# A two-layer hybrid trunk on one core: the routing stretch ahead of the experts written in another order, and a 15th place in the ring of expert weights

## The reference, cut to what matters

```python
def reference(x, ...):                       # x: (1, 256, 1024) float32
    for i in range(2):
        h = rms_norm(x, norm_g[i, 0])
        y = pool_mixer(h, ...) if i % 2 == 0 else forgetting_attention(h, ...)
        x = x + rms_norm(y, norm_g[i, 1])
        h = rms_norm(x, norm_g[i, 2])
        y = swiglu(h, ...) if i % 2 == 0 else moe_swiglu(h, ...)
        x = x + rms_norm(y, norm_g[i, 3])

def moe_swiglu(h, w_router, w_gate, w_up, w_down):
    logits = h @ w_router                    # (256, 8)
    top_val, top_idx = lax.top_k(logits, 2)
    top_w = softmax(top_val)
    gates = sum(one_hot(top_idx, 8) * top_w[..., None])
    for e in range(8):                       # w_gate[e], w_up[e]: 1024 x 3584; w_down[e]: 3584 x 1024
        out = out + gates[..., e:e+1] * ((silu(h @ w_gate[e]) * (h @ w_up[e])) @ w_down[e])
```

## Time and profile before

| what | value |
|---|---|
| median of 3 runs | 1231.81 us (1231.67 to 1235.57) |
| profiled execution: its own time | 1235.62 us |
| profiled execution: span of the trace | 1233.8 us |
| PE busy | 1201.3 us, 97% of the span |
| DVE busy | 686.5 us, 56% |
| ACT busy | 539.6 us, 44% |
| mean DMA rate over the span | 335 GB/s |
| chain of work that ended last | PE 85%, DVE 7%, DMA 6% |

### The profile page before, as it was taken

One profiled execution on the slowest core, in us unless ns is written; L12 is line 12 of the kernel. 1 busy time (PEld: TensorE's weight loads), 2 busy tenths in 40 slices (PEclk: granted clock), 3 DMA queues, 4 the chain that ended last, 5 costly groups with the idle time before them and its releaser, 6 DMA issues.

```text
span 1233.8 us, 15258 instructions
## 1 busy us (share of the span) xinstructions
PE 1201.3 (97%) x5922; PEld 845.5 (69%) x5922; DVE 686.5 (56%) x761; ACT 539.6 (44%) x525; POOL 144.0 (12%) x141
## 2 busy tenths in 40 slices
PE   9999999989989999999999999999999999999996
PEld 8888887778878888434788833578883357887332
DVE  4844455646577988101888710288861038895102
ACT  3743334445546776002677500267750036774001
POOL 0000000000025460100006020000602000050200
PEclk9999999999989999999999999999999999999999
DMA  9955553653376999899999999999999999999994
GB/s 296 361 184 192 180 195 116 198 185 109 109 279 244 370 364 366 334 420 421 422 422 421 419 393 419 423 422 423 419 408 392 420 422 423 422 419 387 397 421 189
DMA packets 128279, 413.52 MB, mean 335 GB/s; under 512 B 10753, under 2 KB 30209, under 8 KB 113794
## 3 DMA queue, kind: packets, MB, share of 16 engines
q1 hardware_dynamic: 127394, 409.28, 85.2%
q0 software_dynamic: 816, 3.28, 0.8%
HBM read 411.48 MB, written 1.05 MB: 334 GB/s over the span
## 4 chain that ended last, share of the span: by engine, by line
PE 85%; DVE 7%; DMA 6%; ACT 1%; SPq 1%; issue 1%; DVEq 0%; ACTq 0%
PE bank L1480 19%; PE bank L1482 19%; PE bank L1481 19%; PE bank L1862 14%; DMA raw<-in_moe_w_gate 5%; PE bank L1875 4%; DVE raw_lo L972 3%; PE bank L1814 1%; PE bank L1942 1%; PE bank L1896 1%; PE bank L1487 1%; SPq L582 1%; DMA head_row<-in_heads 1%; PE bank L1738 1%; DVE y L1391 1%
## 5 line engine op out<-in xcount | busy, mean ns | idle before, releaser
L972 DVE TENSOR_TENSOR raw_lo<-raw,w_hi 128x2048 fp32r<-128x2048 f32 x148 | 337.9, 2303 | 72.1 <-ACT w_hi L641 71.6
L641 ACT ACTIVATE w_hi<-raw 128x2048 fp32r<-128x2048 f32 x149 | 284.5, 1917 | 122.1 <-PE bank L1482 75.7
L1480 PE MATMUL bank<-w_hi,h_hi 128*128 128x512 f32 x568 | 226.4, 399 | 9.8 <-DVE h_lo L1335 5.3
L1481 PE MATMUL bank<-raw_lo,h_hi 128*128 128x512 f32 x576 | 225.0, 391 | 0.0
L1482 PE MATMUL bank<-w_hi,h_lo 128*128 128x512 f32 x568 | 222.6, 392 | 0.0
L1862 PE MATMUL bank<-raw,h_b 128*64 128x512 f32 (+1 forms) x768 | 143.1, 523 | 0.0
L1480 PEld LDWEIGHTS bank<-w_hi,h_hi 128*128 128x128 f32 x568 | 107.1, 189 | 40.7 <-issue 11.5
L1481 PEld LDWEIGHTS bank<-raw_lo,h_hi 128*128 128x128 f32 x576 | 108.7, 189 | 21.9
L1482 PEld LDWEIGHTS bank<-w_hi,h_lo 128*128 128x128 f32 x568 | 106.9, 188 | 23.2
L972 DVE TENSOR_TENSOR raw_extra_lo<-raw_extra,w_hi 128x2048 fp32r<-128x2048 f32 x48 | 112.9, 2372 | 14.6 <-ACT w_hi L641 14.4
L1862 PEld LDWEIGHTS bank<-raw,h_b 128*64 128x64 f32 x768 | 53.6, 137 | 82.5 <-issue 73.9
(11 more groups left out here) (320 smaller groups left out, 1624.4 us busy)
## 6 DMA issues: line engine op xcount, KB each, us to landing
raw<-in_moe_w_gate SPq DMA_DIRECT2D x96, 1024.0 KB, 13.6
raw<-in_moe_w_up SPq DMA_DIRECT2D x80, 1024.0 KB, 14.4
raw<-in_moe_w_down SPq DMA_DIRECT2D x64, 1024.0 KB, 13.9
raw_extra<-in_moe_w_down SPq DMA_DIRECT2D x48, 1024.0 KB, 16.1
raw_extra<-in_moe_w_up SPq DMA_DIRECT2D x32, 1024.0 KB, 12.5
raw_extra<-in_moe_w_gate SPq DMA_DIRECT2D x16, 1024.0 KB, 10.4
raw<-in_ffn_w_gate SPq DMA_DIRECT2D x11, 1024.0 KB, 5.3
raw<-in_ffn_w_up SPq DMA_DIRECT2D x11, 1024.0 KB, 5.0
```

The lines of the kernel that those rows point to most:

```text
L641: nc.scalar.activation(to, raw_slot(source), ACT.Copy).then_inc(hi_ready, 1)
L972: nc.vector.tensor_tensor(lo_slot(source), raw_slot(source), high.bitcast(f32), ALU.subtract).then_inc(lo_ready, 1)
L1480: mm(out, a_hi, b_hi, start=first, stop=False)
L1481: mm(out, a_hi, b_lo, start=False, stop=False)
```

## The change

It has two parts. The first writes the routing in another order: `mboth` is marked for both blocks at once, the gain multiplication of `xn` moves for three quarters from POOL to DVE, the whole low part of the first unit comes behind `sel`, the experts' order and the gates are worked out behind the low part of the first expert's fourth unit and beyond, POOL clears `y` only when the first tokens are split (`he_lo_done` 2), and the router's and the ranking's products repeat their 8 columns 16 times to make 128. The counts of `keep_warm` change. The second gives the ring a 15th place, over `h_lo`, which is free when the attention's projections are done; the split tokens move to `h_e`, over `h_hi`. 84 units are not a multiple of 15 places, and the places are dealt out afresh for each pair (unit j of a pair has place j % 15).

```diff
-EXTRA_SLOTS = 4
+EXTRA_SLOTS = 5
...
-EXPERT_RING = [j % (RAW_SLOTS + EXTRA_SLOTS) for j in range(ROUND_UNITS)]
-assert ROUND_UNITS % (RAW_SLOTS + EXTRA_SLOTS) == 0
+PAIR_UNITS = 2 * ROUND_UNITS
+EXPERT_RING = [j % (RAW_SLOTS + EXTRA_SLOTS) for j in range(PAIR_UNITS)]
...
-WARM = (8, 6, 0, 8, 0, 4, 6)
+WARM = (8, 6, 4, 4, 3, 5, 6)
...
+        with nc.sbuf_tensor("h_e", [P, 2, KB, P], f32r) as h_e:
+            pass
...
-        with nc.sbuf_tensor("x_sq", [P, TB, D], f32) as x_sq:
+        with nc.sbuf_tensor("raw_h", [P, UNIT], f32) as raw_h:
+            pass
+        with nc.sbuf_tensor("raw_h_lo", [P, UNIT], f32r) as raw_h_lo:
             pass
...
-            place = EXPERT_RING[j % ROUND_UNITS]
+            place = EXPERT_RING[j % PAIR_UNITS]
...
         def moe_last(j):
 
-            return max(i for i in range(j - ROUND_UNITS, j) if moe_slot(i) == moe_slot(j))
+            return max(i for i in range(j - PAIR_UNITS, j) if moe_slot(i) == moe_slot(j))
...
         def raw_slot(s):
-            return raw[:, s, :] if s < RAW_SLOTS else raw_extra[:, s - RAW_SLOTS, :]
+            if s == RAW_SLOTS:
+                return raw_h[:, :]
+            return raw[:, s, :] if s < RAW_SLOTS else raw_extra[:, s - RAW_SLOTS - 1, :]
...
-                    sp.wait_ge(*[(unit_used, OUT_U0 + 1), (unit_used, MOE_U0), (x_done, 6),
+                    sp.wait_ge(*[(unit_used, OUT_U0), (unit_used, OUT_U0 + 1), (unit_used, MOE_U0), (x_done, 6),
                                  (x_done, 6)][EXPERT_RING[j] - RAW_SLOTS])
...
-                nc.scalar.activation((x_sq if n == 6 else xn)[:, tb, :], x[:, tb, :], ACT.Square,
+                    sc.wait_ge(sq_done, sq_at(6, 0))
+                nc.scalar.activation(ye[:, :] if n == 6 else xn[:, tb, :], x[:, tb, :], ACT.Square,
...
-
-            def lo_half(u, half):
-                cols = slice(half * (UNIT // 2), (half + 1) * (UNIT // 2))
-                ve.wait_ge(hi_ready, u + 1 - WHOLE_UNITS)
-                step = nc.vector.tensor_tensor(lo_slot(slot_of(u))[:, cols], raw_slot(slot_of(u))[:, cols],
-                                               hi_slot(u)[:, cols].bitcast(f32), ALU.subtract)
-                if half == 1:
-                    step.then_inc(lo_ready, 1)
...
-            def top_two(tb):
+            def top_found(tb):
                 ve.wait_ge(lg_psum, tb + 1)
                 link(nc.vector.tensor_copy(lg[:, tb, :], bank[4 + tb][:, 0:E]))
                 link(nc.vector.max(top[:, tb, :], lg[:, tb, :]))
                 link(nc.vector.max_index(topi[:, tb, :], top[:, tb, :], lg[:, tb, :]))
-                link(nc.vector.tensor_copy(topf[:, tb, :], topi[:, tb, 0:2]))
-                for i in range(2):
-                    step = nc.vector.tensor_scalar(m12[:, tb, i, :], iota8, topf[:, tb, i:i + 1], None, ALU.is_equal)
-                link(step)
-                nc.vector.tensor_tensor(mboth[:, tb, :], m12[:, tb, 0, :], m12[:, tb, 1, :],
-                                        ALU.add).then_inc(m_done, 1)
-
-            top_two(0)
-            lo_half(MOE_U0, 0)
-            top_two(1)
+
+            top_found(0)
+            gain_landed(6)
+            nc.vector.tensor_tensor(xn[:, 1, :], x[:, 1, :], gain[:, 0, :], ALU.mult).then_inc(xn_done, 1)
+            nc.vector.tensor_tensor(xn[:, 0, HALF:D], x[:, 0, HALF:D], gain[:, 0, HALF:D], ALU.mult).then_inc(xn_done, 1)
+            top_found(1)
+            link(nc.vector.tensor_copy(topf[:, :, :], topi[:, :, 0:2]))
+            link(nc.vector.tensor_tensor(m12[:, :, :, :], iota8[:, None, None, :].to_broadcast([P, TB, 2, E]),
+                                         topf[:, :, :, None].to_broadcast([P, TB, 2, E]), ALU.is_equal))
+            nc.vector.tensor_tensor(mboth[:, :, :], m12[:, :, 0, :], m12[:, :, 1, :], ALU.add).then_inc(m_done, 1)
             root(6, 0, TB)
-            ve.wait_ge(m_done, 2)
+            ve.wait_ge(m_done, 1)
             link(nc.vector.tensor_scalar(away[:, :, :], mboth[:, :, 0:1], float(-2 * T), float(2 * T),
                                          ALU.mult, ALU.add))
 
             ve.wait_ge(rank_psum, 1)
...
             link(nc.vector.tensor_tensor(pos0[:, :, :], rank_ps[:, :, 0:1], away[:, :, :], ALU.add))
             for tb in range(TB):
                 nc.vector.tensor_scalar(sel[:, tb, :], iota, pos0[:, tb, :], rstd[:, 6, tb:tb + 1],
                                         ALU.is_equal, ALU.mult).then_inc(sel_ready, 1)
-            lo_half(MOE_U0, 1)
+            lo(MOE_U0)
+            nc.vector.tensor_copy(rank[:, :, :], rank_ps).then_inc(rank_copied, 1)
+            ve.wait_ge(rank_psum, 2)
+            nc.vector.tensor_copy(count, bank[4][:, 0:E]).then_inc(rank_copied, 1)
...
@@ -1332,8 +1339,8 @@
             def he_lo(p, ahead=0, halves=range(2)):
                 for i in halves:
                     ve.wait_ge(he_hi_done, p * 2 + (2 * ahead + i + 1))
-                    nc.vector.tensor_tensor(h_lo[:, 4 * i:4 * i + 4, 0:P], bank_blocks(3, 6 + i),
-                                            h_hi[:, 4 * i:4 * i + 4, 0:P].bitcast(f32),
+                    nc.vector.tensor_tensor(h_e[:, 1, 4 * i:4 * i + 4, :], bank_blocks(3, 6 + i),
+                                            h_e[:, 0, 4 * i:4 * i + 4, :].bitcast(f32),
                                             ALU.subtract).then_inc(he_lo_done, 1)
...
 
-            ve.wait_ge(rank_psum, 2)
-            link(nc.vector.scalar_tensor_tensor(key, count, float(E), tie, ALU.mult, ALU.add))
-            link(nc.vector.tensor_tensor(ahead[:, :, :], key[:, None, :].to_broadcast([P, E, E]),
...
-            link(nc.vector.tensor_tensor_scan(incl, big, big, 0.0, ALU.add, ALU.bypass))
-            nc.vector.tensor_scalar(rtab_i[:, 0:1], incl[0:1, E - 1:E], float(PAIRS), None,
-                                    ALU.add).then_inc(pairs_done, 1)
             lo(MOE_U0 + 3)
-            nc.vector.tensor_copy(rank[:, :, :], rank_ps).then_inc(rank_copied, 1)
-            ve.wait_ge(gexp_done, 1)
-            link(nc.vector.tensor_scalar(gtmp[:, :, 2:3], gtmp[:, :, 1:2], 1.0, None, ALU.add))
-            link(nc.vector.reciprocal(gate[:, :, 0:1], gtmp[:, :, 2:3]))
-            nc.vector.tensor_tensor(gate[:, :, 1:2], gate[:, :, 0:1], gtmp[:, :, 1:2], ALU.mult).then_inc(gates_done, 1)
...
+            def shares():
+                ve.wait_ge(rank_copied, 2)
+                link(nc.vector.scalar_tensor_tensor(key, count, float(E), tie, ALU.mult, ALU.add))
...
+                link(nc.vector.tensor_scalar(small, place, float(PAIRS), None, ALU.is_ge))
+
+            def shares_rest():
+                link(nc.vector.tensor_scalar(cap, small, float(CAP_B - CAP), float(CAP), ALU.mult, ALU.add))
...
+                nc.vector.tensor_scalar(rtab_i[:, 0:1], incl[0:1, E - 1:E], float(PAIRS), None,
+                                        ALU.add).then_inc(pairs_done, 1)
+
+            def gate_shares():
+                ve.wait_ge(gexp_done, 1)
...
+                if is_pair(p, 0):
+                    shares()
+                    lo_to(AHEAD)
+                    shares_rest()
+                    lo_to(AHEAD + 2)
+                    gate_shares()
                 lo_to(last_up(0) + 2)
                 gated_halves(0)
...
+                    if tb == 1:
+                        keep_warm(WARM[2 + 2 * i])
                     pe.wait_ge(*((x_done, 5), (x_done, 5), (x_front, 1), (x_done, 6))[2 * tb + i])
...
+            def repeated(columns):
+                return columns[:, None, :].to_broadcast([P, P // E, E])
+
             def router(tb):
                 for k in range(KB):
                     if k % 4 == 0:
                         pe.wait_ge(x_t_done, 2 * tb + k // 4 + 1)
-                    step = mm(bank[4 + tb][:, 0:E], x_t[:, k, tb * P:(tb + 1) * P], wr_g[:, k, :], start=(k == 0),
-                              stop=(k == KB - 1))
+                    step = mm(bank[4 + tb][:, 0:P], x_t[:, k, tb * P:(tb + 1) * P], repeated(wr_g[:, k, :]),
+                              start=(k == 0), stop=(k == KB - 1))
...
             keep_warm(WARM[5])
 
-            pe.wait_ge(m_done, 2)
+            pe.wait_ge(m_done, 1)
             ones, before = consts[:, C_ONES:C_ONES + P], consts[:, C_TRIS:C_TRIS + P]
-            mm(bank[5][:, 0:E], before, mboth[:, 0, :], start=True, stop=True)
-            mm(bank[5][:, E:2 * E], ones, mboth[:, 0, :], start=True, stop=False)
-            mm(bank[5][:, E:2 * E], before, mboth[:, 1, :], start=False, stop=True).then_inc(rank_psum, 1)
-            mm(bank[4][:, 0:E], ones, mboth[:, 0, :], start=True, stop=False)
-            mm(bank[4][:, 0:E], ones, mboth[:, 1, :], start=False, stop=True).then_inc(rank_psum, 1)
+            both = [repeated(mboth[:, tb, :]) for tb in range(TB)]
+            mm(bank[5][:, 0:P], before, both[0], start=True, stop=True)
+            mm(bank[5][:, P:2 * P], ones, both[0], start=True, stop=False)
```

(40 more changed lines are left out.)

38 lines of the change are left out of this document (20 added, 18 removed).

## The result

The changed kernel takes 1218.2 us (median of four runs, 1216.9 to 1219.5); the kernel before takes 1232.7 on the same chip. The ratio is 0.9876, 95% interval 0.9853 to 0.99, so between 12 and 18 us faster. The forecast was 1221. The profiled execution took 1219.5 us, with a span of 1217.7.

A forecast was written before the change was run, and what follows sets the result against it. PE and DMA were taken as near balance, ring depth deciding, with the routing waiting on small DVE steps. Routing 8.0, 15th place 5.3 and clock 1.5 took 14.8 us off 1235.62: 1220.8, set at 1221, range 1216.5 to 1227.5.

The forecast's parts named there:

- The routing's length: Routing up to the first expert: PE starts it at 368.5 in place of 375.83, gain 7.3 us.
- POOL's first step: Routing, root of block 1: POOL's multiplication of xn, halved to 512 columns, lets DVE's addition end earlier, gain 0.85 us.
- POOL's second step: Routing, search and marks: POOL's second multiplication, 2.36 us, lies over DVE's cast, 1.89 us, and compares, 2.39 us.
- The 15th place: Three changes from "b" to "a" experts: one more unit in flight removes PE's waits, gain 5.3 us, lower end 2.5.
- the sum: Whole kernel: 8.0 + 5.3 + 1.5 = 14.8 us off the profiled 1235.62, giving 1220.8; median set at 1221.
- The clock term: Behind the third change: PE at clock 0.50 from 1011 to 1014 us, half lost, counted as 1.5 us gained.
- The 0.7 us behind the third unit: First expert: PE's wait at 384.69, 0.7 us behind three units' end, came from the experts' order and goes.
- The lead on landing: At the three changes: units land some 7 to 8 us before PE's first product.
- The slower rival: Ring places dealt out afresh: unit 84 waits for unit 75, PE stands 6.5 us at each change, 1241.8; chance 0.05.
- The clearing: First expert: POOL's clearing of y beside DVE's low parts; forecast 0 us, rival 1.7 us, 1222.5, chance 0.13.
- the rival that did so: Whole kernel: the 3.8 us between profiled execution and median stay, 1217; chance 0.07.

The follow-up runs named there:

- the order alone: Changed kernel with router and ranking products of 8 columns again and the old keep_warm counts: 1224.8 us, ratio 0.9928.
- new_routing_14: Changed kernel with the new routing but a ring of 14 places: 1224.6 us, ratio 0.9929 to the kernel before the change.
- before: The kernel without the change, against which all ratios are taken: median 1232.7 us, profiled execution 1235.62 us.
- after: The changed kernel with both parts, against the kernel before: median 1218.2 us, ratio 0.9876, profiled execution 1219.5 us.
- old_routing_15: Kernel with the old routing and only the ring's part of the change, 15 places: 1226.9 us, ratio 0.9942 to the kernel before the change.
- old_order_128: Changed kernel with the old routing order on DVE and POOL, keeping PE's 128-column products, new keep_warm counts and 15 places: 1225.8 us, ratio 0.994.
- short_start: Changed kernel with the next "a" expert's fourth low part ahead of the additions to y, and twelve keep_warm instructions removed from the start: 1216.7 us.
- eight_columns: Changed kernel with router and ranking products of 8 columns again, keep_warm counts left as changed: 1221.0 us, ratio 0.9885.

## Why the prediction was right, and where it was not

**The routing's length held.** 7.3 us were predicted and 7.3 measured; seen from the router's start, which was 1.1 us earlier, gather and first expert came 0.2 us before and 0.1 us behind their predicted places (364.9 for 365.1, 368.6 for 368.5). Clock 1.00 throughout, and cast and compare near 0.2 us, came as said.

**How the routing's steps were told apart was too simple.** The prediction followed one path with both halves of the change in place and charged the old length to POOL's steps and to the clock, each for itself. PE's part alone gives 2.5 us, the order alone 2.8, both 7.2. DVE's long cast and compares cost also the clock of what comes behind PE's stand, and this second cost was in no term. The gain of 0.85 for POOL's first step measured 0.65. POOL's second step, which the text charged with cast and compares, costs nothing once the cast comes behind the second search.

**The 15th place held.** The three waits are gone, and one place less brings back 5.1 us of waiting and 1.7 of half clock, where the sum had 5.3 and 1.5. The clock term was read from one window; the windows beside it have 0.99 and 0.94, which makes the 1.5 us 1.7. The 0.7 us behind the third unit went with the new routing: the experts' stretch of new_routing_14 is 0.9 us shorter than that of before, and after's 0.5 shorter than that of old_routing_15. Only 0.41 us of the 0.7 was a wait (timeline of before). The stream no longer sets the pace: units land 778.27 - 568.08 = 210.2 us apart and PE starts 784.74 - 574.34 = 210.4 apart, the 210.5 forecast. Where the second "a" expert ends, 12 us moved 386 GB/s in the earlier trace rows; in after no 12 us there move less than 415. The lead on landing, said to be 7 to 8 us, was 6.3. The prediction's own terms give 5.9 (4.94 and the 0.93 in hand), so that sign was worked out wrongly, and the time does not rest on it.

**The slower rival fell, but not by much.** Its geometry came as worked out: unit 84 went out when PE was done with unit 75. The 12.30 us for which ACT waited in the timeline above end with its landing. SP's timeline of after:

```profile
555.53 6.36 SPq L594 DMA_DIRECT2D raw<-in_moe_w_gate  x4
```

The view merges four issues; the first is this transfer. It landed at 568.08, 12.5 us later and not the 19.0 that the rival took from the earlier trace rows. The prediction's own answer to the rival, some five units ahead of it in the stream and so 12.3 us of work, fits. From landing to first product the split needs 4.94 us, so 6.3 leave 1.3 in hand. With 13 places the same release comes three units later, and PE does wait there, but with the stream at its full rate.

**The clearing did not stop DVE.** In after it stood at 370.88, beside two low parts of the ordinary length:

```profile
369.89 2.28 DVE L984 TENSOR_TENSOR raw_lo<-raw,w_hi 128x2048 fp32r<-128x2048 f32 x1
372.47 2.29 DVE L984 TENSOR_TENSOR raw_lo<-raw,w_hi 128x2048 fp32r<-128x2048 f32 x1 [0.30 <-ACT w_hi L653]
```

The rule of the Trainium skill (SBUF — State Buffer, SBUF: two separate sides) that a DVE step with two inputs in SBUF is locked out only by a GpSimd step that reads SBUF agrees with all three rows: the clearing beside low parts, the clearing beside multiplications, and POOL's multiplication beside the sums, which alone of the three made DVE wait. The cast that the prediction set beside this rule has one input and tests only the lock. Nor is the clearing harmless to every DVE step. In old_order_128 it runs from 358.61 to 360.47, over two compares with one input tensor each, and they end with it at 360.50, after 2.37 us; the same two take 0.36 there when POOL is quiet.

**What was wrong is the step from the profile to the median.** The prediction held that half clock in the routing and behind the third change was most of the 3.8 us between the profiled execution and the median, and set the new median at the sum. But the new profiled execution is free of both, and still stands 1.3 us above its median. What differs between executions is the start, by up to 3.7 us. Both of these two profiled executions had the slow one. Leaving out short_start, five traces have it, and in them the first router starts at 353.0 to 354.2 us; in the other seven it starts at 349.2 to 351.4, though nothing of the change lies ahead of it. So the median should have been set below the sum; the rival that did so gave 1217, and the measured median is between the two. The forecast came within 3 us because the sum off the profile, 14.8, holds: the two profiled executions differ by 16.1, of which 1.1 is not the change's. That the two profiled executions had the same start is luck. That the start alone explains the spread of the medians is argued from the traces, not shown: the unprofiled runs have none.

## What to carry to other kernels

Where two streams are near balance, count one more place in the ring as at least one unit's transfer at each point where the stream is late, until the surplus covers the wait. Here that gave 7.4 us for a place and 9.4 to 9.5 were measured, since waits inside the experts and half clock come on top. Then look at what is late next, which here was DMA again after PE had gained 2.6 us. A chain of small steps costs twice: once for its length, and once for the clock of the products behind it; fix the chain and fill PE with wide products together, since each alone gave little more than a third of the whole. Before a median is forecast from one profiled execution, compare the start of two traces.

## What the runs showed that was not expected

Behind products of 8 columns the clock falls even when PE has no gap: 0.53 with 3.00 of 3.00 us busy in eight_columns, where it is 1.00 once these products have 128 columns. At the start of a kernel identical instructions take 2.86 us or 1.53, by the execution, with a granted clock of 1.00 on record in both. And a place that comes free out of its turn lets its transfer go out 12.2 us before it lands, where 20.8 are usual, but the stream keeps its rate meanwhile.
